# Row items' down projection as pairs of 256 weight columns, one term of each unit cut at 320

## The reference

```python
def moe_swiglu(h, w_router, w_gate_e, w_up_e, w_down_e):
    ...
    logits = (xt @ w_router).astype(jnp.float32)
    top_val, top_idx = lax.top_k(logits, TOP_K)
    gates = jax.nn.softmax(top_val, axis=-1)
    ...
    hg = lax.ragged_dot(xs, w_gate_e, sizes)
    hu = lax.ragged_dot(xs, w_up_e, sizes)
    ys = lax.ragged_dot(jax.nn.silu(hg) * hu, w_down_e, sizes)
    ys = ys * gates.reshape(-1)[order][:, None].astype(ys.dtype)
    out = jnp.zeros_like(xt).at[tok].add(ys)
```

## Time and profile before

| quantity | before |
| --- | --- |
| median of three runs | 3488.38 us |
| profiled execution | 3493.34 us |
| its span, first to last instruction | 3491.8 us |
| PE busy | 3442.3 us, 25495 matmuls |
| PE weight loads busy | 3243.7 us |
| DVE busy | 2043.4 us |
| ACT busy | 1563.0 us |
| mean granted TensorE clock | 0.993 of full |
| matmuls of 512 weight columns on `mah`, `mal` | 3 x 560 |

### The profile page before, as it was taken

The page is one execution under the profiler, slowest core; times in us unless marked ns, Lnnn a source line. Parts: engine busy times, 40 slices in busy tenths (PEclk is TensorE's granted clock), DMA queues, the critical chain, the costliest instruction groups (busy, mean ns, idle before and its releaser), DMA issues.

```text
span 3491.8 us, 68944 instructions
## 1 busy us (share of the span) xinstructions
PE 3442.3 (99%) x25495; PEld 3243.7 (93%) x25495; DVE 2043.4 (59%) x3129; ACT 1563.0 (45%) x2335; POOL 221.4 (6%) x259
## 2 busy tenths in 40 slices
PE   9999899999999999999999999999999999999998
PEld 8888799999999899799999999999999898898886
DVE  6455577766544556454455455446555587686774
ACT  4455433333333433354344344445454465554653
POOL 1000000000100000022010001001010020010100
PEclk9999899999999999999999999999999999999999
DMA  5111332222553423266455445456566575665654
GB/s 199 38 51 41 137 117 73 85 83 84 200 186 117 137 67 110 105 201 182 152 183 193 163 164 200 164 168 228 192 223 207 187 244 195 202 231 190 228 198 155
DMA packets 159181, 548.23 MB, mean 157 GB/s; under 512 B 23345, under 2 KB 23353, under 8 KB 159056
## 3 DMA queue, kind: packets, MB, share of 16 engines
q1 hardware_dynamic: 123248, 444.67, 38.8%
q0 software_dynamic: 32352, 95.54, 7.8%
q10 hardware_dynamic: 3456, 6.29, 0.5%
HBM read 508.20 MB, written 59.08 MB: 162 GB/s over the span
## 4 chain that ended last, share of the span: by engine, by line
PE 96%; DVE 2%; ACT 1%; issue 1%; DMA 0%; DVEq 0%; SPq 0%; POOL 0%; POOLq 0%; ACTq 0%
PE ps L342 77%; PE ps L2494 8%; PE ps L2495 4%; PE ps L738 1%; PE ps L809 1%; PE ps L821 1%; PE ps L2418 1%; PE ps L839 0%; PE ps L829 0%; ACT eA L878 0%; DMA yT<-in_xT 0%; PE ps L762 0%; PE ps L1207 0%; PE ps L1994 0%; PE ps L2448 0%
## 5 line engine op out<-in xcount | busy, mean ns | idle before, releaser
L328 DVE TENSOR_TENSOR wl<-wraw,wh 128x1024 fp32r<-128x1024 f32 x800 | 979.3, 1225 | 887.1 <-ACT wh L324 878.0
L324 ACT ACTIVATE wh<-wraw 128x1024 fp32r<-128x1024 f32 x796 | 841.0, 1057 | 930.0 <-PE ps L342 867.1
L342 PE MATMUL ps<-ex,wh 128*128 128x256 f32 (+2 forms) x4484 | 850.7, 289 | 1.1 <-DVE wl L328 1.1
L342 PEld LDWEIGHTS ps<-ex,wh 128*128 128x128 f32 x4484 | 704.4, 188 | 1.5 <-issue 1.4
L342 PE MATMUL ps<-ex,wl 128*128 128x288 f32 (+2 forms) x2240 | 647.1, 289 | 0.0
L2494 PE MATMUL ps<-ex,wh 128*128 128x480 f32 x1344 | 445.2, 382 | 0.0
L342 PEld LDWEIGHTS ps<-ex,wl 128*128 128x128 f32 x2240 | 420.6, 188 | 0.0
L342 PE MATMUL ps<-xs,wh 128*128 128x256 f32 x2432 | 388.9, 282 | 4.3 <-DVE qAl L865 1.9
L342 PE MATMUL ps<-bc,wh 128*128 128x256 f32 (+1 forms) x2496 | 386.6, 277 | 0.0
L2495 PE MATMUL ps<-ex,wl 128*128 128x240 f32 x1344 | 366.5, 273 | 0.0
L342 PEld LDWEIGHTS ps<-xs,wh 128*128 128x128 f32 x2432 | 327.0, 190 | 15.9 <-issue 9.9
(11 more groups left out here) (390 smaller groups left out, 4773.9 us busy)
## 6 DMA issues: line engine op xcount, KB each, us to landing
wraw<-in_w_expert SPq DMA_DIRECT2D x676, 512.0 KB, 3.3
wraw<-in_w_main SPq DMA_DIRECT2D x164, 512.0 KB, 3.8
act_d<-ast POOLq DMA_DIRECT2D x22, 512.0 KB, 2.9
araw<-act_d POOLq DMA_DIRECT2D x22, 512.0 KB, 5.1
hT<-h_d POOLq DMA_DIRECT2D x4, 2048.0 KB, 14.3
h_d<-hT POOLq DMA_DIRECT2D x3, 2048.0 KB, 9.6
hT<-in_xT POOLq DMA_DIRECT2D x2, 2048.0 KB, 9.6
xrow_d<-rows ACTq DMA_DIRECT2D x16, 256.0 KB, 2.1
```

Source lines behind the costliest of these rows:

```text
L324: act.activation(wh[:, j], wraw[:, j], ACT.Copy).then_inc(hi_done, 1)
L328: dve.tensor_tensor(wl[:, j], wraw[:, j], wh[:, j].bitcast(F32), ALU.subtract).then_inc(lo_done, 1)
L342: mm = pe.matmul(out[:, s], a, b[:, s], start=first and part == 0 and c == 0, stop=last and part == 2 and d == n)
```

## The change

The call of `product` in `down_rows_pe` loses `wide=True`, so each term becomes two matmuls of 256 columns, and gains a cut for the first term of each unit's first product:

```diff
@@ -2457,7 +2457,7 @@
                         ch, cl = (a[:, 2 * u + ff, P * tb:P * tb + P] for a in (mah, mal))
                         w = slice(512 * ff, 512 * ff + 512)
                         mm = product(pe, bank(b + tb), ch, cl, wh[:, j, w], wl[:, j, w],
-                                     first and ff == 0, last and ff == 1, wide=True)
+                                     first and ff == 0, last and ff == 1, cuts=EVEN if ff == 0 and tb == 0 else None)
                 mm.then_inc(unit_used, 1)
```

## The result

The changed kernel takes 3509.74 us, the median of six runs (3507.61 to 3511.74), against 3489.31 us for six runs of the kernel before (3486.91 to 3493.9). The ratio is 1.0056 (95% interval 1.0043 to 1.0069): 20.4 us slower. The forecast was 3491.2 us with a range of 3484 to 3501, so it was wrong, and the time lies outside the range. Rival 1 had foreseen 14.4 us of the loss. The rest is mostly something that no part of the prediction speaks of.

A forecast was written before the change was run, and what follows sets the result against it. The prediction took TensorE's matmul start distances as the bound. A unit of 24 x 113.33 + 47 = 2767 ns against 2747, times 140, gave +2.8 us on 3488.4: 3491.2 us, range 3484 to 3501.

The forecast's parts named there:

- Rival 1: Row items' down projection: pairs stay at the slow pace despite cuts, +14.4 us, 3502.8 us; chance 0.13.
- What bounds the kernel: Whole program: TensorE, busy 99% of the span, is one matmul stream, so distances between matmul starts set the length.
- The cut's price: Each unit's 320/192 cut in the down projection: 47 ns at the quick pace, about 23 in a slow stream.
- Rival 2: Down projection: quick pace and a cut costing only 5 ns, -3.1 us, 3485.3 us; chance 0.13 including mixtures with the forecast.
- The paces: Matmuls of 256 columns start every 113.3 ns (quick) or 117.8 ns (slow), at the same granted clock.
- Rivals 3 and 5: Down-projection pairs: 3, starts every 109 ns, 3476.6 us, chance 0.08; 5, every added start costs, 3498.7 us, chance 0.04.
- Which pace will hold?: Down projection: with one cut per unit, the quick pace was expected in nearly all of 140 units.
- rows 9 and 10: Layer 0 trace evidence: 18 cut rounds entered and left quick; one cut mended a slow stretch, another did not.
- its bounds: Down projection, operands swapped and cuts 24 apart: pace between 109 and 117.8 ns, cut between about 5 and 47 ns.
- Where streams start: Down projection: 15 starts or resumptions after transposes lose at most one slow unit each, 1.2 us in all.
- Rival 4: The 240-token items' gate-and-up stretch, now behind pairs, turns slow: +11.8 us besides +2.8, 3503 us; chance 0.04.

## Why the prediction was wrong

- **What bounds the kernel: right.** PE's start distances set everything. PE was never idle for DVE or ACT in a half.
- **The cut's price: right.** 47 ns at the quick pace, measured 46 among 512-column matmuls here and 45 in layer 0 with seven times as many; 24 ns in a slow stream, as said. Rival 2, a cut for 5 ns, is out.
- **The paces: right.** 113.3 and 117.8 ns are the only two that appeared, with weights moving too. Rivals 3 and 5 are out: no pair at 109 ns a matmul, none at 115 to 116. (The Trainium skill's rule for a warm matmul, "TensorE: Matmul & The Clock Gate", "Back-to-back issue gap", gives 109.2 for 256 columns; no stream of 256-column matmuls in these runs went so fast. The section calls the rule that of an isolated matmul, which the prediction left out, and gives about 131 ns for 512 columns in a stream; the 228.9 measured here lie near neither.)
- **"Which pace will hold?": wrong.** This is the step that failed. It took the cut for a means that brings or keeps the quick pace, from rows 9 and 10, all of one stage. There it is true, even seven times as dense. In the row items the first cut ends the quick pace (39.87 against 38.08 us), and in slow streams it brought no recovery in any of the 140 units. The sum was +14.0 us where the forecast had +2.8: rival 1, which had said 14.4, with its condition (more than two units in five slow) met in all 140. Its chance of 0.13 was too low. Of the 14.0 us, 8.1 are there without any cut: the pairs kept the slow pace in 112 units, where the forecast had them quick and 27 ns a unit shorter than before. The other 5.9 came with the cuts, 3.6 of them in the 28 units whose quick pace they ended. "Against: no slow stretch in the trace outlived two cuts" rested on very few cases, all in one stage with the operands' roles exchanged: the cut at 539.55, another at 493.60 that also brought the quick pace, and the one at 516.91 that didn't. The prediction names that exchange under its bounds, and there it let it move the price of a cut and the pace, but not the effect of a cut on the pace.
- **Where streams start: wrong.** At 15 places I took no more than one lost unit each. Without any cut, the streams behind the transposes and all in the 240-token items came in slow and stayed so. Even with no cut, only 28 of the 140 units were quick.
- **The length of the code: missed.** 672 more instructions in a loop body that is run twice made PE wait 2.36 us for its program and then run for 3 us at half of the granted clock: 4.2 us. The sum had no term for it. The prediction said that no wait moves, and looked at the other engines only. The page of before had the row for it (86 packets on queue 8), and the number of instructions was there to be counted.
- **Rival 4: did not happen.** The 240-token items' gate and up took 148.34 us before and after. Its condition, a slow pace of that stream, does exist: 149.33 us in two of the runs, 1.0 us an item, where the rival had put 11.8 us on three.

The sum of what the traces show is 14.0 + 4.2 = 18.2 us. Of the measured 20.4, 2.2 us are left, which the two profiled runs don't hold and the spread of the runs (4 to 7 us) covers.

No version tried beats the kernel before. The best, pairs in the first halves of the 256-token items, saves 0.38 us twice in its trace, and its ratio is 1.0.

## What to carry to other kernels

A matmul stream can have two stable paces at one and the same clock. In most places here it kept the one that it came in with, but the same code also ran at either, and a remedy seen in one stage has to be measured again in the next, above all where the operands change roles. Splitting matmuls also doubles the code: before a loop body grows, count its instructions against the longest body that the trace shows coming round without a fetch; beyond that, look at the instruction queue and at PE's idle time where the loop starts again. Rows that all come from one stretch are one observation, however many they are.

## What the runs showed that I had not expected

- The two paces of 256-column matmuls, 113.33 and 117.78 ns, differ by 4.45 ns and hold over thousands of matmuls. They can pass from one stage into the next across a change of operand. The stream of 480 and 240 columns has two as well. A cut of 320 and 192, one matmul of 512 among pairs, or two `sum_pe` matmuls ended the quick one in row-wise streams; a cut of 128 and 384 never did, and sometimes brought it.
- A cut of 128 and 384 costs 70 ns (2.79 us against 2.72 a unit), one of 320 and 192 costs 46 or 47, and 24 in a slow stream.
- Going back in a loop whose body is 1762 instructions or longer cost 2.0 to 4.7 us between the two 256-token items. It was either one halt of 2.4 to 2.8 us and then some 3 us with the granted clock at half, or two halts, of 0.4 to 3.0 us and then 1.1, with the clock at full.
- The same code can take either pace: of three 240-token items that run one loop body, one was quick in a half and two were slow.
